# Squares on ScalarE, value halves ahead of the next mask, a new order at the opening, and the first expert rows by product

## The reference, cut to what matters

```python
def first_block(x, c, positions, ...):
    cos, sin = rope_tables(positions)
    c_act = silu(c)
    for l in range(2):
        mod = c_act @ w_ada[l] + b_ada[l]                 # 6 x 1024 modulation values
        h = rms_norm(x, g_mix[l]) * (1 + sc_m) + sh_m
        qa, ka, va, qi, ki, wi, qb, kb, vb, ga, gb = split_cols(h @ w_in[l] + b_in[l])
        qa, ka = partial_rope(rms_norm(qa)), partial_rope(rms_norm(ka))   # per head of 64
        y_a = sparse_indexed_attention(...) @ w_oa[l]     # 8 heads, one key head, the 128 best keys by qi, ki, wi
        qb, kb = rms_norm(qb), rms_norm(kb)
        y_b = chunked_band_attention(qb, kb, vb, rel_bias[l]) @ w_ob[l]   # 8 heads
        x = x + gt_m * ((sigmoid(ga) * y_a + sigmoid(gb) * y_b) @ w_out[l])
        x = x + gt_f * feed_forward(modulated rms_norm(x))
    return x

def second_block(x, c, ...):
    h = modulated layer_norm(x)
    mix = hybrid_mixer(h)        # forgetting attention (16 heads), multiscale pool, state space mixer
    x = layer_norm(ALPHA * x + g_m * mix)
    h = modulated layer_norm(x)
    ffn = grouped_moe(h)         # router over 16 experts in 4 groups, 2 experts per token
    return layer_norm(ALPHA * x + g_f * ffn)
```

## Time and profile before

| | us |
|---|---|
| median of three timed executions | 3482.54 |
| profiled execution, own time | 3475.47 |
| its span, first to last instruction | 3473.9 |
| TensorE busy | 3122.5 (90%) |
| VectorE busy | 1463.7 (42%) |
| GpSimd busy | 1096.8 (32%) |
| ScalarE busy | 1057.7 (30%) |

### The profile page before, as it was taken

How to read it: one execution, slowest core, us unless ns; L and a number is a source line. 1 busy time by engine, 2 the same in 40 slices (tenths; PEclk the granted TensorE clock), 3 DMA queues, 4 the chain that set the end, 5 groups by cost and what they waited for, 6 DMA issues and landing times.

```text
span 3473.9 us, 39011 instructions
## 1 busy us (share of the span) xinstructions
PE 3122.5 (90%) x15454; PEld 2403.8 (69%) x15454; DVE 1463.7 (42%) x2564; ACT 1057.7 (30%) x1646; POOL 1096.8 (32%) x539
## 2 busy tenths in 40 slices
PE   3987899999888789899997999989999966999995
PEld 2664777887766567688775767867777735888883
DVE  6677573212167757422203436647673250000003
ACT  3444324223244442422314442223443230000002
POOL 1231243444323214344443553434443401000001
PEclk8998999999999889999998999999999988999997
DMA  5110463433321026374232226443332307889883
GB/s 208 56 48 31 153 201 108 141 126 97 100 79 55 31 104 212 103 290 145 88 109 82 80 67 218 134 121 109 110 104 85 109 0 301 336 336 334 331 325 109
DMA packets 186036, 501.72 MB, mean 144 GB/s; under 512 B 19408, under 2 KB 101456, under 8 KB 175776
## 3 DMA queue, kind: packets, MB, share of 16 engines
q1 hardware_dynamic: 162048, 415.14, 35.8%
q0 software_dynamic: 13344, 49.84, 3.7%
q10 hardware_dynamic: 10496, 34.71, 2.9%
HBM read 464.36 MB, written 35.29 MB: 144 GB/s over the span
## 4 chain that ended last, share of the span: by engine, by line
PE 74%; DVE 14%; ACT 4%; DMA 3%; issue 2%; POOL 1%; ACTq 1%; DVEq 0%; SPq 0%; POOLq 0%
PE banks L652 17%; PE banks L654 17%; PE banks L653 17%; PE banks L1219 9%; PE banks L1241 5%; PE banks L709 2%; DMA ring<-in_w_all 2%; PE banks L755 1%; PE banks L734 1%; DVE arena L2053 1%; PE banks L744 1%; DVE arena L2052 1%; PE banks L715 1%; DVE abuf L1933 1%; DVE rstd L1891 1%
## 5 line engine op out<-in xcount | busy, mean ns | idle before, releaser
L2579 POOL TENSOR_TENSOR w_lo<-ring,w_hi 128x1024 fp32r<-128x1024 f32 (+1 forms) x379 | 919.9, 2429 | 1499.2 <-ACT w_hi L1334 1498.9
L653 PE MATMUL banks<-h_lo,w_hi 128*128 128x512 f32 x2104 | 838.1, 398 | 0.0
L652 PE MATMUL banks<-hx_hi,w_hi 128*128 128x512 f32 (+2 forms) x1400 | 587.6, 420 | 51.1 <-DVE h_lo L1886 32.8
L1334 ACT ACTIVATE w_hi<-ring 128x1024 fp32r<-128x1024 f32 (+1 forms) x379 | 392.8, 1038 | 606.4 <-DMA ring<-in_w_all 515.5
L654 PE MATMUL banks<-hx_hi,w_lo 128*128 128x512 f32 (+2 forms) x1400 | 557.7, 398 | 0.0
L653 PEld LDWEIGHTS banks<-h_lo,w_hi 128*128 128x128 f32 x2104 | 403.1, 192 | 95.1 <-issue 9.2
L652 PEld LDWEIGHTS banks<-hx_hi,w_hi 128*128 128x128 f32 (+2 forms) x1400 | 270.3, 193 | 150.7 <-issue 79.5
L1219 PE MATMUL banks<-abuf,ring 128*128 128x128 f32 x2944 | 334.6, 276 | 1.4 <-DVE abuf L2530 0.9
L1219 PEld LDWEIGHTS banks<-abuf,ring 128*128 128x128 f32 x2944 | 332.3, 193 | 1.9 <-issue 1.9
L654 PEld LDWEIGHTS banks<-hx_hi,w_lo 128*128 128x128 f32 (+2 forms) x1400 | 269.1, 192 | 61.0 <-issue 0.4
L652 PE MATMUL banks<-hf_hi,w_hi 128*128 128x512 f32 x704 | 278.4, 395 | 14.3 <-DVE h_lo L1886 14.3
(11 more groups left out here) (377 smaller groups left out, 4520.7 us busy)
## 6 DMA issues: line engine op xcount, KB each, us to landing
ring<-in_w_all SPq DMA_DIRECT2D x356, 512.0 KB, 3.9
ring<-in_w_all SPq DMA_DIRECT2D x46, 2048.0 KB, 8.1
arena<-in_w_all SPq DMA_DIRECT2D x27, 2048.0 KB, 8.5
arena<-in_w_all SPq DMA_DIRECT2D x80, 512.0 KB, 5.3
abuf<-in_w_all SPq DMA_DIRECT2D x48, 512.0 KB, 4.7
routed<-abuf POOLq DMA_DIRECT2D x1, 12288.0 KB, 50.3
abuf<-routed POOLq DMA_DIRECT2D x24, 512.0 KB, 8.5
made<-abuf POOLq DMA_DIRECT2D x23, 512.0 KB, 7.9
```

Source lines behind the costliest of these rows:

```text
L652: pe.matmul(bank[0:m, :], upper, hi, start=first, stop=False)
L653: pe.matmul(bank[0:m, :], upper, lo, start=False, stop=False)
L1334: act.activation(w_hi[s][:, 0:n], raw_w[s][:, 0:n], ACT.Copy).then_inc(w_upper, 1)
L2579: pool.tensor_tensor(w_lo[s][:, 0:n], raw_w[s][:, 0:n], w_hi[s][:, 0:n], ALU.subtract)\
```

## The change

Four groups of edits.

1. Opening: one semaphore for each input; `cond` is loaded first; SyncE issues three modulation loads first, then two weight units, the fourth modulation load in two halves, then the third unit. ScalarE squares `x` at once. VectorE does the angles after the second group of reductions, and the reciprocal before the last four; the squaring of the cosine moves behind the normalisation of `ka`. ScalarE does the sine after the root.
2. `square` moves from VectorE to ScalarE, each right behind the `take` of its tile (only that of `qa3` waits until step 18); `head_normed` uses `tmp` instead of `sq`.
3. `upper_values` and `values_of` stand ahead of the step's exponential and mask, in both blocks.
4. Router: one counter `router_step` takes the place of eight semaphores; the weights' normalisation goes to the end; the memset goes ahead of the router. VectorE makes a one-hot matrix of the tokens of block 0, and TensorE makes the transposed rows of block 0 as 32 products of `htok` with it. GpSimd's loads begin with block 1, and `rows_in(1)` stands behind `up_block(0, 0)`.

```diff
 # SyncE
-            load(3)
             for i in range(4):
                 _, ((at, size), _) = next(ada)
-                sp.dma_start(ada_first[:, 4 * i * D:4 * (i + 1) * D], ...).then_inc(sem("first%d_in" % i), 16)
+                if i == 3:
+                    load(2)
+                    sp.dma_start(ada_first[:, 12 * D:14 * D], src[:, 0:2 * D]).then_inc(sem("wada_in3"), 16)
+                    sp.dma_start(ada_first[:, 14 * D:16 * D], src[:, 2 * D:4 * D]).then_inc(sem("last_in"), 16)
+                else:
+                    sp.dma_start(ada_first[:, 4 * i * D:4 * (i + 1) * D], src).then_inc(sem("wada_in%d" % i), 16)
+            load(1)
 # TensorE
+            def first_rows():
+                router_told(pe, "rows_chosen")
+                for k in range(KC):
+                    for t in range(QT):
+                        mm = pe.matmul(pt_b[k // 4][:, (k % 4) * P:(k % 4 + 1) * P], htok[:, t, k * P:(k + 1) * P],
+                                       chosen_rows[:, t, :], start=(t == 0), stop=(t == QT - 1))
+                mm.then_inc(sem("rows_turned"), 1)
...
-            rows_in(0)
+            first_rows()
             gate_block(0, 0)
+            up_block(0, 0)
             rows_in(1)
-            up_block(0, 0)
 # ScalarE
-            for dst, src in ((cst[:, :], consts), (csil, cond[:, 0:D]), (raw[0].bitcast(I32), pos_in),
-                             (x[:, :, :], x_in), (vec2[:, :], vec2_all)):
-                act.dma_start(dst, src).then_inc(boot, 16)
+            act.dma_start(csil, cond[:, 0:D]).then_inc(sem("cond_in"), 16)
+            act.dma_start(cst[:, :], consts).then_inc(sem("cst_in"), 16)
+            act.dma_start(x[:, :, :], x_in).then_inc(sem("x_in"), 16)
+            act.dma_start(pts[1].bitcast(I32), pos_in).then_inc(boot, 16)
+            act.dma_start(vec[:, :], vec1_all[0:P * NV1].rearrange("(p n) -> p n", p=P)).then_inc(vec_in, 16)
+            act.dma_start(vec2[:, :], vec2_all).then_inc(sem("vec2_in"), 16)
...
-            act.wait_ge(boot, 80)
+            act.wait_ge(sem("cond_in"), 16)
             act.activation(csil, csil, ACT.Silu).then_inc(sem("c_ready"), 1)
+            act.wait_ge(sem("x_in"), 16)
+            for k in range(KC):
+                act.activation(h[:, k, :], x[:, k, :], ACT.Square).then_inc(sem("x_squared"), 1)
...
                 root(1.0 / D, EPS, at("norm1", "aux"))
+                if layer == 0:
+                    ...
+                    load_vectors(0)
+                    upper_to(1)
+                    act.wait_ge(sem("angle_done"), 1)
+                    mine(act.activation(sinT[:, :], tmp[:, :], ACT.Sin))
+                    act.activation(cosT[:, :], tmp[:, :], ACT.Sin, scale=0.5).then_inc(sem("sin_done"), 1)
                 affine(h, layer * 2 * KC, gain_at(0), mod_at(0), sem("h_upper"), hx_hi)
                 if layer == 0:
+                    upper_to(2)
...
+                def square(name):
+                    n = MIX.index(name)
+                    taken(act, at("mix", "lin") + n)
+                    src = raw[(at("mix", "prep") + n) % 2]
+                    act.activation(sq[:, :], src, ACT.Square).then_inc(sem("sq_done"), 1)
...
                 take("ka")
+                square("ka")
...
+                    if r == 1 and j:
+                        upper_values(st + 4 * (j - 1), hi_of(j - 1))
                     if s + 2 < STEPS:
                         exponent(st + s + 2, s + 2)
-                    if r == 1 and j:
-                        upper_values(st + 4 * (j - 1), hi_of(j - 1))
                     if r == 2 and j < 3:
                         take(("qb2", "qb3", "qa0")[j])
+                        square(("qb2", "qb3", "qa0")[j])
 # VectorE
-            dve.wait_ge(boot, 80)
-            ... the angles, the wait for the sine, the cosine ...
             dve.wait_ge(sem("c_ready"), 1)
             hold(dve)
-            for n in range(4):
-                dve.wait_ge(sem("first%d_in" % n), 16)
-                modulate(ada_first[:, 4 * n * D:4 * (n + 1) * D], 4 * n, 4, sem("tiles_read") if n == 3 else None)
+            for n in range(3):
+                dve.wait_ge(sem("wada_in%d" % n), 16)
+                modulate(ada_first[:, 4 * n * D:4 * (n + 1) * D], 4 * n, 4, None)
+                if n == 1:
+                    angles()
+            read(dve, LAYER.at("norm1", "aux"))
+            mine(dve.reciprocal(rstd[:, :], rstd[:, :]))
+            dve.wait_ge(sem("wada_in3"), 16)
+            modulate(ada_first[:, 12 * D:14 * D], 12, 2, None)
+            dve.wait_ge(sem("last_in"), 16)
+            modulate(ada_first[:, 14 * D:16 * D], 14, 2, sem("tiles_read"))
...
-                square("ka")
                 head_normed("ka", kaT, v1("kn_a"), sem("normed"))
+                if layer == 0:
+                    turns_made()
...
+                    if r == 1 and j:
+                        values_of(j - 1)
                     if s + 2 < STEPS:
                         mix_masked(s + 2)
-                    if r == 1 and j:
-                        values_of(j - 1)
-                    if r == 0 and j < 3:
-                        square("kb%d" % (j + 1))
...
             step(TT(gw, e1, e2, ADD))
-            dve.sem_inc(sem("chosen"), 1)
+            dve.sem_inc(sem("router_step"), 1)
... (the weights' eight steps now follow the rows below)
+            dve.sem_inc(sem("router_step"), 1)
+            for t in range(QT):
+                step(TS(chosen_rows[:, t, :], iota, dest1[:, t:t + 1], None, ALU.is_equal))
+                ins = STT(chosen_rows[:, t, :], iota, dest2[:, t:t + 1], chosen_rows[:, t, :], ALU.is_equal, ADD)
+            tell(ins, sem("router_step"))
 # GpSimd
-            load_rows(0)
-            pool.wait_ge(sem("rows_turned"), 1)
             load_rows(1)
```

190 lines of the change are left out of this document (95 added, 95 removed).

## The result

The changed kernel takes 3441.62 us in the median (3438.07 to 3445.02, four executions), the kernel before on the same chip 3484.54. The ratio is 0.9882, with a 95% interval of 0.9869 to 0.9896: 42.9 us less, where 57.5 were forecast. The time lies in the stated range (3403 to 3456), 17 us above the forecast and 5 us from rival (a).

What follows compares the result with a forecast made beforehand. TensorE was taken as the bound (74% of the span on the chain), with time to regain only where it idles. Gains of 5 + 32 + 5 + 15.5 = 57.5 us from 3482.5 gave 3425 us, range 3403 to 3456.

Steps and rivals of the forecast that it cites:

- rival (a): Attention steps: VectorE becomes the bound and freed waits return as waits for masks; gain 36 us, 3446.5 us; chance 0.20.
- Opening: Start to first product: reordered loads and VectorE work let the first tile be scaled earlier; gain 5 us, bounds 0 and 9.
- Squares: Attention steps: 13 squares a layer move to ScalarE at 0.63 us each, ending TensorE's 21.0 us of waits in 8 cases.
- rival (c): Attention steps: squares reload ScalarE's tables, two loads for each of 26 squares, 66.7 us; total 3492 us; chance 0.03.
- Value halves: Attention steps: halves ahead of mask and exponential free the bank sooner; with squares 16 us a layer, 32 for both.
- two first pairs: Block one's attention, waits of 4.18 + 1.94 and 2.7 + 2.9 us: 3.4 us gained at each, the mask coming next.
- late pairs: Block one's attention, three waits for the lower half like the one ending at 330.83: 2.1 us each, 6.3 a layer.
- Block two: Its attention: five waits of about 0.5 us go whole, two of 3.3 give near 1.2 each; 5 us, bounds 2 and 9.
- Experts: Router and first expert rows: copy of choices sooner, 32 products replace block 0's scatter and load; 15.5 us, bounds 11 and 19.
- estimate of 2898: Experts' start: block 1's gate block was to begin near 2898 us instead of 2913.79, once its rows and weights landed.
- Rival (b): Experts' start: block 1's rows or weights land late, leaving 4 us of the lead; gain 46 us, 3436.5 us; chance 0.08.
- three quarters of 21.0 + 39.5: Block one's attention: upper bound on the gain from squares and value halves in both layers, given as 44 us.

Runs made afterwards that it cites:

- opening_by_need: Changed kernel with the opening's loads in order of need, angles behind the first four reductions and reciprocal behind all: 3449.09 us, ratio 0.9909.
- combined: Changed kernel plus gates_lower_behind, weights_behind_rows, opening_by_need's loads (angles behind second group, reciprocal behind third) and ScalarE's evacuation ahead of the exponential: 3413.36 us, ratio 0.9797.
- combined_topk_later: combined with the top-k rounds of the first step of pairs 1 to 3 moved behind the next step's mask: 3412.19 us, ratio 0.9804.
- values_behind: Changed kernel with the value halves again behind the exponential and mask in all three attentions: 3465.66 us, ratio 0.9951.
- squares_back: Changed kernel with the 13 squares a layer back on VectorE at their old places: 3449.5 us, ratio 0.9908.
- changed_again: The changed kernel run once more, unedited, on the chip of two other kernels: 3447.33 us, ratio 0.9893.
- weights_behind_rows: Changed kernel with SyncE asking for the expert loop's first weights only once block 1's rows have landed: 3441.23 us, ratio 0.9879.
- gates_lower_behind: Changed kernel; in the first block's gates VectorE splits the merged tile after reading the two gate banks, not before: 3432.8 us, ratio 0.986.
- rows_by_dma: Changed kernel with block 0's rows scattered, loaded and turned as before, without one-hot operations, keeping the new router order: 3448.0 us, ratio 0.9897.

## Why the forecast was right, and where its steps were not

**Opening, 5 forecast, 4.4 measured: the size right, the working not.** First tile at 50.34, said near 50. But the loads were taken to land otherwise. The positions and `x`, on which the working had no wait, landed at 29 and 27, and VectorE stood 6.67 us for the positions. Against that, the second modulation load, said at 22 and a wait of 4.3 us, cost only 0.68, the first reduction began at 11.40 instead of 12.5, and the loss beside GpSimd was 2.0 us instead of 3.5. That these cancelled is luck. The working shared the DMA evenly by bytes between the two queues; in opening_by_need they shared it by packets, and ScalarE's smaller ones carried a fifth of the bytes. Two reorderings showed that the positions, `x` and its column sums, and the constants come late one behind the other. Only the order of combined, in which VectorE reaches the angles when the constants land (1.15 us of waiting), gave 4 us.

The rule of the Trainium skill (SBUF — State Buffer, Who interferes with whom) would have given 3. What it describes is in the trace: a reduction of two inputs took 3.24 us beside GpSimd and 1.22 alone. The reciprocal, with one input, ran its 3.35 us undisturbed, 2.1 of them beside GpSimd's first split, so the exclusion cost less than the two whole splits counted.

**Squares: the mechanism right, the size known only roughly.** Each takes 0.62 us on ScalarE, TensorE's waits for them are gone but for `ka`'s (1.6 us a layer), and no table load stands in the attention steps: rival (c) is out. The Trainium skill (ScalarE: Activation LUTs, Rules for kernel authors) advises VectorE for multiplies, with a speed for bf16; at this f32 size ScalarE took 0.62 us against 0.69, and moving the squares gained 8.7 to 11.9 us of mixing, so here the measurement speaks against the rule.

**Value halves: the step that failed.** Of 16 us a layer, squares and halves together, 12.2 and 10.7 came, and of these only 3.5 and 6.3 were waits. The prediction gave 3.4 us to each of the two first pairs, "since the mask behind the top-k rounds, moved by about 1 us, comes next". Measured are 6.1 us of waits before and 5.8 after at the first of them, 5.6 and 4.2 + 0.5 at the next: the half itself stood behind the rounds and VectorE's other work, and the freed square only let TensorE come earlier to that wait. It is the mechanism of rival (a) in this stretch, and combined_topk_later shows how little the order can do there. At the late pairs 2.1 each were said, with the scores' wait for the mask as what comes next. That wait is there (0.78), but two more stood behind the delayed mask that the working had not followed: ScalarE's copy behind the exponential, and VectorE's normalisation. TensorE's waits for that copy took back 0.5, 1.5 and 2.8 us, so that the three late pairs gave 1.4 and 0.3 us and nothing. Block two gave 4.9 of 5, for there the five small waits that go whole do most.

**What brought the mixing near its forecast: the clock.** The prediction counts waits alone. By waits the two mixing stages gained 9.8 us of the 32 forecast; 13.0 more came because TensorE ran a smaller part of its work at 1.2 GHz. No term had this, so that the total lies in the range is in part luck: without the 13 us the time would be near 3455 (an estimate: 3441.6 + 13), at the range's edge. Whether fewer and shorter waits raised the clock is not shown. Most profiles fit it (0.89 in values_behind and squares_back, 0.91 and 0.92 in combined), but changed_again has 0.88 in layer 0 with fewer waits than the changed kernel.

**Rival (a)** said 3446.5, with the freed waits coming back as waits for masks. In time the mixing gained 22.8 us where it said 14 and the forecast 32: about halfway. In waits it is nearer: 42.0 us of waits for squares and halves went, and TensorE's idle time in the two mixing stages and block two's attention fell by 14.7. Of the 27 that came back 7.0 are waits for masks, as it said, and 12.9 for ScalarE's copy, which it did not name. The forecast and this rival both worked without the clock, so the total does not decide between them.

**Experts: 15.5 forecast, 9.5 measured.** The products took 10.25 us (10 said); the one-hot operations were done by 2843.5, 10.8 us after the turn of the choices (10.2 said). The term that was mis-sized is the load of block 1's rows: at most 8.5 us from the earlier trace rows, a median over all loads of the kernel; it took 11.2 here, just issued behind two of weights. It was also issued 31.8 us after the turn, where 30.1 were said and 31.5 is the kernel before: the scatter began 1.1 us earlier, but took 1.4 longer to its end. weights_behind_rows shows that neither order of the two loads meets the estimate of 2898 for the gate block: rows alone land early, and then the weights do not. Rival (b), 4 us, was too low.

**What was in no term besides:** 4.3 us lost in the gates of layer 0 and 2.4 behind the experts' start. The first is in the waits named above (4.0 us more idle time of TensorE), and gates_lower_behind took them out together with those that were there before. Why there are more of them than before is not shown. In the second stretch TensorE is idle for 41.2 us as before, and its busy time grew from 518.9 to 521.2 at a granted clock of 0.955 instead of 0.960. The ten profiles with the row products other than combined and combined_topk_later have this (562.1 to 562.8 us); combined, combined_topk_later and rows_by_dma have 560.2 to 560.5 at 0.960.

One bound of the prediction is added wrongly: three quarters of 21.0 + 39.5 are 45, not 44, which moves nothing.

Of the signs set down beforehand, the first tile, the squares and the table loads were met; the lower halves' waits (24.7 us, said under 15) and the lead of block 1 (45.9 us, said near 40) were not. Of the signs of being wrong, the masks' waits grew by 7.0 us where the halves' lost 24.2, and block 1's rows held TensorE for 6.4 us (8.0 in changed_again), where more than 8 was set.

## What to carry to other kernels

When an operation is pulled ahead in an in-order queue, list everything that stood behind the one it overtakes, on its own engine and on the engine that waits for that one in turn; the wait comes back at the last of them, not at the first. Where the stretch shows the engine busy for three quarters of the time or more (VectorE: 87.5 of the 120 us from 160 us on, in the changed kernel), moving work about on it may only move the waits. Split every measured gain into idle and busy time of the engine that bounds the kernel before it is put down to waits: more than half of the mixing's gain here was clock. And look into stages that the change does not touch: reading a bank ahead of an unrelated wait gave 13.8 us here, more than any further reordering of the attention steps, and it was to be seen in the trace of before, as three small waits.

## What the runs showed of the hardware

- Two DMA queues that both had work shared it by packets: 468 and 466 of them from 5 to 25 us in opening_by_need, but 6.88 and 1.67 MB. So 950 KB of constants on the queue of small packets, asked for at 1.92 us, took 21.3 us to land, while the DMA moved 428 GB/s.
- 512 KB of rows take 3.6 us alone, 5.0 with the weights held back, 11.2 behind two 2 MB loads.
- A two-input VectorE operation of 0.69 us took 2.46, and one of 1.28 up to 3.4, while GpSimd split a weight unit (2.4 us). In a stage of 112 VectorE instructions the order of one of them was worth 13 us of VectorE's busy time.
- The same 1258 records of matrix products took 250.7 us of TensorE's busy time in the mixing of layer 0 of the changed kernel, 257.9 in changed_again and 259.4 before: it was busy at the half clock for 44.3, 61.0 and 62.6 us of them.
